# Eight context tiles of the second block's first feed-forward layer made inside the first block's mixer

## The reference

```python
def swiglu_2(x, w1, w3, w2):
    return (jax.nn.silu(x @ w1) * (x @ w3)) @ w2
...
    mod = jax.nn.silu(c) @ w_ada[l] + b_ada[l]
...
    modc = jax.nn.silu(c_ctx) @ w_ada[l] + b_ada[l]
...
    h = h + HALF * gt1 * swiglu_2(ada_norm(h, g_ffn1[l], sh1, sc1), w1_ffn1[l], w3_ffn1[l], w2_ffn1[l])
    hc = hc + HALF * cgt1 * swiglu_2(ada_norm(hc, g_ffn1[l], csh1, csc1), w1_ffn1[l], w3_ffn1[l], w2_ffn1[l])
```

## Time and profile before

| | |
|---|---|
| median of 3 runs | 2664.79 us |
| profiled execution | 2659.51 us |
| its span | 2657.7 us |
| TensorE busy | 2567.2 us (97%) |
| VectorE busy | 1668.7 us (63%) |
| ScalarE busy | 1105.1 us (42%) |
| mean granted TensorE clock | 0.99 |
| moved by DMA | 380.44 MB, 143 GB/s |

### The profile page before, as it was taken

How to read it: one execution, slowest core, us unless ns; L and a number is a source line. 1 busy time by engine, 2 the same in 40 slices (tenths; PEclk the granted TensorE clock), 3 DMA queues, 4 the chain that set the end, 5 groups by cost and what they waited for, 6 DMA issues and landing times.

```text
span 2657.7 us, 38440 instructions
## 1 busy us (share of the span) xinstructions
PE 2567.2 (97%) x15728; PEld 2278.7 (86%) x15728; DVE 1668.7 (63%) x2629; ACT 1105.1 (42%) x1720; POOL 66.1 (2%) x60
## 2 busy tenths in 40 slices
PE   7998898999999999999999999999999999998998
PEld 7998798999888888778888888889888888888998
DVE  6767645777677665656644777655555446776655
ACT  5446654555322224444243422224222225655553
POOL 0001031000000000000000000000000000010000
PEclk9999999999999999999999999999999999999999
DMA  7775202675555543112222455553444423244554
GB/s 260 234 233 183 83 17 68 208 238 178 167 182 186 177 144 100 58 40 72 96 90 84 135 185 179 177 170 113 136 140 139 133 97 133 84 132 157 178 192 148
DMA packets 109536, 380.44 MB, mean 143 GB/s; under 512 B 11952, under 2 KB 15792, under 8 KB 108976
## 3 DMA queue, kind: packets, MB, share of 16 engines
q1 hardware_dynamic: 108352, 372.80, 42.6%
q10 hardware_dynamic: 1008, 5.18, 0.5%
HBM read 376.88 MB, written 1.05 MB: 142 GB/s over the span
## 4 chain that ended last, share of the span: by engine, by line
PE 89%; DVE 5%; ACT 3%; issue 2%; DMA 0%; SPq 0%; ACTq 0%; DVEq 0%
PE B L1497 26%; PE B L1498 25%; PE B L1499 25%; DVE w_lo L2126 2%; ACT w_hi L1819 1%; PE B L1758 1%; PE B L1741 1%; PE B L1512 1%; PE B L1651 1%; PE B L1513 1%; PE B L1664 1%; PE B L1514 1%; PE B L1748 1%; DVE AC L2371 1%; DVE TMP L2153 0%
## 5 line engine op out<-in xcount | busy, mean ns | idle before, releaser
L1497 PE MATMUL B<-U,w_hi 128*128 128x256 f32 (+1 forms) x2896 | 958.3, 331 | 7.7 <-DVE w_lo L2126 7.5
L1498 PE MATMUL B<-U,w_hi 128*128 128x256 f32 (+1 forms) x2896 | 950.1, 328 | 0.0
L1499 PE MATMUL B<-U,w_lo 128*128 128x256 f32 (+1 forms) x2896 | 950.0, 328 | 0.0
L2126 DVE TENSOR_TENSOR w_lo<-w_raw,w_hi 128x1024 fp32r<-128x1024 f32 (+3 forms) x583 | 683.6, 1185 | 391.9 <-ACT w_hi L1819 391.2
L1819 ACT ACTIVATE w_hi<-w_raw 128x1024 fp32r<-128x1024 f32 (+3 forms) x583 | 590.2, 1018 | 491.8 <-PE B L1499 470.4
L1497 PEld LDWEIGHTS B<-U,w_hi 128*128 128x128 f32 x2896 | 545.6, 188 | 64.3 <-issue 7.4
L1498 PEld LDWEIGHTS B<-U,w_hi 128*128 128x128 f32 x2896 | 545.5, 188 | 52.4 <-issue 1.5
L1499 PEld LDWEIGHTS B<-U,w_lo 128*128 128x128 f32 x2896 | 545.5, 188 | 51.9
L1497 PE MATMUL B<-HHf,w_hi 128*128 128x256 f32 (+1 forms) x1122 | 363.8, 324 | 1.7 <-DVE w_lo L2126 1.6
L1499 PE MATMUL B<-HHf,w_lo 128*128 128x256 f32 (+1 forms) x1122 | 362.9, 323 | 0.0
L1498 PE MATMUL B<-HLf,w_hi 128*128 128x256 f32 (+1 forms) x1122 | 362.9, 323 | 0.0
(11 more groups left out here) (355 smaller groups left out, 2537.9 us busy)
## 6 DMA issues: line engine op xcount, KB each, us to landing
w_raw<-in_w SPq DMA_DIRECT2D x504, 512.0 KB, 4.2
w_ada<-in_w SPq DMA_DIRECT2D x144, 512.0 KB, 3.3
w_raw<-in_w SPq DMA_DIRECT2D x58, 384.0 KB, 3.4
w_raw<-in_w SPq DMA_DIRECT2D x8, 320.0 KB, 2.8
X<-in_x SPq DMA_DIRECT2D x2, 1024.0 KB, 9.7
w_raw<-in_w SPq DMA_DIRECT2D x8, 256.0 KB, 2.7
BW<-in_bias ACTq DMA_DIRECT2D x1, 1536.0 KB, 10.3
K<-in_consts ACTq DMA_DIRECT2D x2, 640.0 KB, 4.5
```

The source lines that it names most:

```text
L1497: pe.matmul(o, hi, xh, start=i == 0 and s.start, stop=False)
L1498: pe.matmul(o, hi, xl, start=False, stop=False)
L1499: e = pe.matmul(o, lo, xh, start=False, stop=i == last and s.stop)
L2126: dve.tensor_tensor(w_lo[:, plan.slot[u], 0:n], w_raw[:, plan.ring[u], 0:n], w_hi[:, plan.slot[u], 0:n].bitcast(F32), ALU.subtract).then_i ...
```

## The change

Tiles 14 to 21 (`FIRST` to `NF - 1`) of f10 are made for the context alone outside f10: tile 14 at the border between f1 and the mixer, tiles 15 to 20 as tasks `x15` to `x20` of the mixer's first part, tile 21 at the border before f2. In f10 these tiles stream only the 256 token columns; their weights are loaded and split a second time.

For that, the normalized context is needed earlier. Its sum of squares is taken during f1, and its norm (`nc`) at the end of f1, written into `UC`, which lies over `CS` and `w_ada`. The first 16 `ada` steps stand in f1, and no `ada` step runs between f1 and the second tiles of f2. The results go into the context half of `X`. After tile 21, in f2, two row blocks and `CS` are loaded again, the Silu of `CS` is made again, the results are moved to `HB`, and the context half of `X` is loaded again. `ADA10` gives f10's `ada` steps turn by turn.

```diff
-ADA = {"f1": 12, "f2": 12, "f10": 48, "f20": 48, "f11": 24, "f21": 0}
-ADAS = {"f1": 28, "f2": 25, "f10": 27, "f20": 27, "f11": 27, "f21": 28}
+ADA = {"f1": 16, "f2": 8, "f10": 48, "f20": 48, "f11": 24, "f21": 0}
+ADAS = {"f1": 25, "f2": 25, "f10": 27, "f20": 27, "f11": 27, "f21": 28}
+FIRST = 14
+ADA10 = [2] * (FIRST - 1) + [1, 0] * ((NF - FIRST) // 2) + [3, 3, 3, 3, 2, 2, 2]
...
+    def ffn(self, p, n, begun, gate, old, stat=None, beside=None, aside=iter(())):
+        turns, share = 0, lambda i: sum(ADA10[:i]) if p == "f10" else min(i * ADA[p] // ADAS[p], ADA[p])
...
+            cols = 256 if p == "f10" and j >= FIRST else n
+            g, u = (begun.get((p, x, j)) or self.gemm((p, x, j), self.tile(p, x, j), cols) for x in "gu")
...
+            self.add("ffn_h", key=(p, j), n=cols, b=g, b2=u, t=t, need=old, arg=cols < n)
...
+            next(aside, None)
...
+    def context(self, roots):
+        for _ in range(9):
+            yield
+        stat = Stat(self, "c0", 256)
+        for k in range(8):
+            stat.add_("XC", k, ("x2", 0))
+            yield
+        for _ in range(5):
+            yield
+        roots.append(stat.rsqrt(D, o=256))
+        for _ in range(6):
+            yield
+        half = self.ada_half("nc", 0, 0, ("ada", (0, 15)), "UC", 1, roots[0])
+        for some in (4, 4):
+            for _ in range(some):
+                next(half)
+            yield
+    def restore(self):
+        yield
+        self.add("rows", need=(("mm", ("fc", "u", NF - 1)),))
+        self.add("cs_load", need=(("mm", ("fc", "u", NF - 1)),))
+        self.add("cs", key=1)
+        self.add("hb", need=(("hm", ("fc", NF - 1)), ("mm", ("wout", 7))))
+        for _ in range(3):
+            yield
+        self.add("x_again", need=(("x2", "hb"),))
+    def fill(self, j):
+        need = tuple(("ul", ("nc", k, 1)) for k in range(8))
+        wts = [self.weights(self.tile("f10", x, j)) for x in "gu"]
+        b, b2 = self.PS.get(), self.PS.get()
+        self.gemm(("fc", "g", j), None, 256, x="UC", need=need, wts=wts[0], b=b)
+        yield
+        self.gemm(("fc", "u", j), None, 256, x="UC", need=need, wts=wts[1], b=b2)
+        t = self.TM.get()
+        self.add("fill_h", key=("fc", j), b=b, b2=b2, t=t)
...
+    def border(self, stat, j, pieces):
+        work = self.fill(j)
+        next(work)
+        wts = self.fetch(pieces)
+        rb = stat.rsqrt(D)
+        next(work)
+        return stat, rb, wts
...
-        order = "c0 c1 q0 q4 v b0 b1 o0 c2 c3 q1 q5 b2 b3 o1 c4 c5 c6 c7 s0 s1 q2 q6 b4 b5 o2 u0 u1 u2 u3 k0 k1 q3 q7 b6 b7 o3 c8 c9 c10 c11 s2 d w0 w1 g0 g1"
+        order = "c0 c1 q0 q4 v b0 b1 x15 o0 c2 c3 q1 q5 b2 b3 x16 o1 c4 c5 c6 c7 s0 s1 x17 q2 q6 b4 b5 x18 o2 u0 u1 u2 u3 k0 k1 q3 q7 b6 b7 x19 o3 c8 c9 c10 c11 s2 d w0 w1 g0 g1 x20"
...
-        for _ in rounds([*[delta(o, d) for o in range(2) for d in range(2)], gates(), context()], 6):
+        for _ in rounds([*[delta(o, d) for o in range(2) for d in range(2)], gates()], 6):
```

On the engines, `ffn_h` of these eight tiles has one more copy on ScalarE and one more difference on VectorE for the context half; `fill_h` has a Silu on ScalarE and a product on VectorE:

```diff
+                if s.arg:
+                    w.wait_ge(*at("x2", "hb"))
+                    act.activation(HI[p][:, j, 256:512], HB[:, j - FIRST, :], ACT.Copy)
...
+                if s.arg:
+                    w.wait_ge(*at("x2", "hb"))
+                    dve.tensor_tensor(LO[p][:, j, 256:512], HB[:, j - FIRST, :], HI[p][:, j, 256:512].bitcast(F32), ALU.subtract)
```

More of the change, by code:

```diff
@@ L360, in ada @@
             self.last_ada = (l, b)
-            if b % 24 == 23:
+            if (l, b) in ((0, 15), (0, 23)):
+                self.add("derive", key=(0, 0), arg="gate" if b == 23 else "norm")
+            elif b % 24 == 23:
                 self.add("derive", key=(l, b // 24))
@@ L449, in whole @@
         need = self.norm_to_u("ffn1_norm", rb, None)
-        self.add("cs")
+        self.add("cs", key=0)
         keys = [("f1", "g", 0), ("f1", "u", 0)]
-        stat = self.ffn("f1", 256, dict(zip(keys, self.pair(keys, wts, 256, need))), None, ())
-        wts = self.fetch([("win", k, 128 * j, 128) for k in range(8) for j in range(2)])
-        rb = stat.rsqrt(D)
+        roots = []
+        stat = self.ffn("f1", 256, dict(zip(keys, self.pair(keys, wts, 256, need))), None, (), aside=self.context(roots))
+        rc = roots[0]
+        stat, rb, wts = self.border(stat, FIRST, [("win", k, 128 * j, 128) for k in range(8) for j in range(2)])
         need = self.norm_to_u("mix_norm", rb, self.lastU)
-        rc, stat = self.mix1(wts, need)
-        wts = self.fetch(self.first_of("f2"))
-        rb = stat.rsqrt(D)
+        stat = self.mix1(wts, need)
+        stat, rb, wts = self.border(stat, NF - 1, self.first_of("f2"))
         need = self.norm_to_u("ffn2_norm", rb, self.lastU)
@@ L557, in gates, with fill @@
             self.add("exp_table")
[L559 to L569, removed]
+        def fill(j):
+            yield from PS.room(2)
+            yield from TM.room()
+            work = self.fill(j)
+            next(work)
+            yield split + (("P", 2750),)
+            yield from TM.room()
+            next(work)
+            yield split + (("P", 2750), ("A", 2950), ("D", 420))
         def decay():
@@ L1356, in program @@
     hidden("f2", 256)
+    with ExitStack() as st:
+        sb("HBgap", [128, 21792], F32, st)
+        HB = sb("HB", [128, 8, 256], F32, st)
     hidden("f10", 512)
@@ L1441, in delta, with half @@
         return i, d, C(tri), C(st_), lm, um, gq, IT, UU, T_, P_, Y, UL_
+    def half(s):
+        return slice(0, 256) if s.x == "UC" else slice(s.o, s.o + 256)
     def neg(s):
@@ L2147, in vector @@
                 w.each(s.t.after)
+                if s.key[0] == "n10" and h:
+                    w.wait_ge(*at("x2", 1))
                 if k == "anorm":
@@ L2155, in vector @@
             elif k == "anorm_lo":
[L2156 removed]
+                (l, i), (_, j, h) = s.arg, s.key
                 w.wait_ge(*at("uh", s.key))
                 dve.scalar_tensor_tensor(
[L2159 to L2160 removed]
+                    out=LO[s.x][:, j, half(s)], in0=TM(s.t, 256), scalar=MOD[:, l, 24 * i + j, h:h + 1],
+                    in1=HI[s.x][:, j, half(s)].bitcast(F32), op0=ALU.add, op1=ALU.subtract).then_inc(*up("ul", s.key))
             elif k == "ffn_h":
```

96 lines of the change are left out of this document (63 added, 33 removed).

## The result

The changed kernel takes 2701.34 us (median of 4 runs, 2698.59 to 2706.14) against 2662.01 us before (median of 4, 2658.33 to 2680.1): **slower** by 1.4%, ratio 1.0143, 95% interval [1.0116, 1.0169]. That is clear of the noise, though under 2%. It lies above the forecast's range, 2636 to 2667, and also above the 2673 of all terms at their high ends; slower had been given a chance of 0.02. The profiled execution's span is 2696.8 us, 39.1 longer than before, and the mean granted clock 0.985 (before 0.990).

A forecast was written before the change was run, and what follows sets the result against it. TensorE was taken as the bound, busy 2567.2 of 2657.7 us. Terms -43.1 (f10), +1.2 (its VectorE), +1.0 (f1), +1.2 (borders), +20.5 (mixer) and +9.0 (reload) gave -10.2 from 2659.5: 2649.3 us, range 2636 to 2667.

The forecast's parts named there:

- It won't be filled whole: Mixer's first part: six tiles' 32.5 us of matmuls fill 12 of 18 us of room; +20.5, between +14.5 and +29.5.
- Rival B: Mixer's first part is bound by its chains and the tiles lengthen them; +7.8 in all, 2667 us; chance 0.12.
- The borders: Around the mixer: gate and up products cover the norm's wait, TensorE never idles; +0.6 each, +1.2 both, bounds 0 and +4.
- The reload in f2: ScalarE stands for the reloaded `CS`, and TensorE waits for a weight split behind its Silu; +9.0, bounds 0 and +13.
- f10: Eight tiles go from 512 to 256 columns, -43.1 us; a lag of VectorE in four of them, +1.2.
- unless that cover fails: f10's down turn: three `ada` steps have 14.9 us of TensorE over them and cost nothing; bound +5.
- C's sign: Rival C: TensorE waits in f10's eight tiles, 2653 us, within the forecast; sign: under 430 starts in 50 us.
- f1: +1.0, bounds 0 and +3: f1: four more `ada` steps, eight sums and the context's norm on VectorE make TensorE wait; +1.0.
- D, the weight load laid bare: Rival: a 256-column matmul of these tiles takes the weight load's 188 ns instead of 112.9; 2700 us; chance 1 in 100.

The follow-up runs named there:

- run 2: Changed kernel with the six mixer tiles' work left out but their places in the planner kept; ratio to before 1.0014, mixer's stretch 132.0 us (before 119.0).
- run 10: Changed kernel, order kept, with all splits and loads of the six mixer tiles but one matmul in place of each 24; ratio to before 1.0140.
- run 1: Changed kernel with the Silu of the eight context tiles replaced by a copy; ratio to before 1.0132, mixer's stretch from 166.9 to 161.4 us.
- run 4: Changed kernel with the two border tiles' Silu and product behind the norm; ratio to before 1.0149, borders 16.1 and 16.7 us instead of 16.9 and 17.0.
- run 3: Changed kernel with the Silu of the reloaded `CS` two tiles later in f2; ratio to before 1.0119, f2 from 193.6 to 183.5 us.
- run 12: Changed kernel with the view `U1` moved 192 bytes further on, to the place of `U0`; ratio to before 1.0238.
- run 6: Kernel before with four `ada` steps moved from f2 to f1, f1's spread over 25 turns; ratio to before 1.0003, f1 202.5 us.

## Why the prediction was wrong

The forecast was -10.2 us, the profile shows +39.1. The gap of 49.3 is 27.4 in the mixer, 7.5 at the borders, 7.5 in f10, 5.7 in f1 and 4.9 in f2, less 3.7 in the chains and the rest.

- *"It won't be filled whole ... I take 12, two thirds; bounds 3 and 18."* The step that failed. Filled were less than none: 47.9 us for 32.5 of matmuls (34.6 at the 120 ns that they take from `UC`). Even the bound of +29.5 was 18.4 short. I put room (15.0 of idle time) against work, as if the idle time stood still. It is the latency of chains that run through all three engines; the planner's new order alone adds 13.0 (run 2), and the tiles 34.9 on top. By run 10 the tiles without their products make 15.9 of idle time, and the products fill 19.3.
- *Rival B* named the right mechanism, gave it 0.12 and priced it at 38.5. Against it I held that "VectorE idles 52 us there, so that the long wait at least should take a tile". That argument was wrong: run 10 adds no products and TensorE's idle time grows by 15.9, though VectorE is busy 100 of 160 us. B had also no price for the clock, up to 15.0 us lost at the low one against 3.6 before, and none for the new order.
- *Table loads*, eleven more at 1283 ns in the mixer's stretch, are missing from the sum. They are worth some 5 us there (run 1).
- *The borders: "TensorE never idles, so the clock should stay"*. It idles 1.98 and 0.62 to 0.63 at each. I had the norm start 2.5 us after Ln as before, and overlooked `fill_h`, whose product on VectorE waits for the up product ahead of the norm. The split that I priced at +0.6 stands inside the norm and not in front of it: with `fill_h` out of the way (run 4) TensorE waits 2.0 there, and the border gains under 1 us. +8.7 against +1.2.
- *The reload in f2: +9.0.* Right, in place and size: TensorE stood 9.33 (8.7 in the text), and run 3 took 10.1 off. f2 lost 13.9 because two things came on top: 2.9 us lost in 5.8 at 1.2 GHz, which I had at "up to 1.5", and a second wait of 1.4, with ScalarE waiting 3.37 for a weight unit that SP issued behind the second load of `X`, which I had at "nothing, +2 if not".
- *f10: -43.1, and 1.2 back.* -34.4. The 1.2 was put on the short tiles, which have no wait. Two waits stand elsewhere: 2.3 where the two `ada` steps of a long tile meet the first short one, with the clock behind it, and 2.0 in the last down product, against *"nothing, unless that cover fails"*. And a 256-column matmul from `U1` takes 120 ns, not the 112.9 of `U0` in f1 (384 x 7.1 ns = 2.7 us; run 12). The row that I priced it from reads another view: from `U1` two halves take 240 ns and the whole 226.7, so the cut isn't free. C's sign, under 430 starts in 50 us, came (418), but by this pace and not by C's wait.
- *f1: +1.0, bounds 0 and +3.* +6.7, of it 4.8 for four `ada` steps (run 6): not by waits, as I had costed them, but by a wider spacing of all matmuls.
- *D, the weight load laid bare*, fell: spacings of 113 to 120 ns at full clock where it had 188. The Trainium skill (TensorE: Matmul & The Clock Gate, "Back-to-back issue gap") gives 131 ns at 512 columns for a stream of weight loads and matmuls. The traces here do not agree, with 226.7 and 233.3; its 81 ns at 128 columns no stream here can test.

The cause is shown by runs for the mixer and the reload, and read from the trace for f10's waits. Open are why more `ada` steps widen the spacing in f1, why the place of the operand changes it, and what the border costs without the split inside its norm.

## What to carry to other kernels

Work moved into another stage gains only what it fills there, and idle time between dependent steps on three engines is not room: price the moved work on every engine that the chain runs through, or put it in one block, where here a tile cost 5.67 us instead of 8.0. A tile halved in f10 saved 5.1 by its pitch (10.88 less 5.76) and 4.3 in the stage's measured time, so that even the block could not win. Where a written order or a planner decides, run the new order once without the work; here that told 13 of the 48 us.

## What the runs showed of the hardware

- Matmuls of 256 columns stream at full clock at three even spacings: 113.3 ns (5.44 us for 48), 117.7 (5.65) and 120 (5.76). `UC` and `U1` gave 120; `U0` gave 113.3 or 117.7, and in run 6 changed from one to the other inside f1, behind a single longer tile, and stayed. When `U1` was moved by 192 bytes, every second short tile took 5.44 and the others 5.91, and at 512 columns 226.7 ns (10.88) became 233.3 (11.20).
- After an idle time of 5.88 us TensorE ran at 1.2 GHz for over 8 us; after one of 9.33 for some 5.8. A long wait costs more than itself, and the profile books the second part as busy time.
- A switch of ScalarE's function table takes 1283 ns, and the next function starts right behind it (520.46 to 521.75).
